# Interleaving the recurrent heads more densely with the input projection, with three rows of the working buffer laid out anew

## The reference, cut to what matters

```python
h = _rmsnorm(x, mix_norm_gain[l])
proj = h @ w_in[l]                                   # 1696 RWKV columns, 1536 attention columns
p_rwkv, p_attn = proj[..., :RWKV_COLS], proj[..., RWKV_COLS:]
y_rwkv = _rwkv7_mixer(p_rwkv, ...)                   # 8 heads of 64, a recurrence over the tokens
q, k, v = (t.reshape(B, S, ATTN_HEADS, HEAD_DIM) for t in jnp.split(p_attn, 3, axis=-1))
q = _partial_rotary(q, positions)
k = _partial_rotary(k, positions)
o = _dilated_attention(q, k, v)                      # 8 heads of 64, causal, three dilated patterns
o = _rmsnorm(o, ...)
x = x + jnp.concatenate([y_rwkv, y_attn], axis=-1) @ w_out[l]
```

## Time and profile before

| | us |
|---|---|
| median of three runs (3556.31 to 3567.62) | 3562.47 |
| the profiled execution, its own time | 3562.47 |
| its span, first to last instruction | 3560.6 |
| TensorE busy in it | 3266.1 (92%) |
| VectorE busy | 1754.1 (49%) |
| ScalarE busy | 1186.1 (33%) |
| mean granted clock of TensorE, as a share of 2.4 GHz | 0.958 |
| projection, second half, to the last tile's step | 1933.5 to 2222.3 |
| rest of the heads, to the first matmul of the output projection | 2222.3 to 2731.3 |

### The profile page before, as it was taken

How to read it: one execution, slowest core, us unless ns; L and a number is a source line. 1 busy time by engine, 2 the same in 40 slices (tenths; PEclk the granted TensorE clock), 3 DMA queues, 4 the chain that set the end, 5 groups by cost and what they waited for, 6 DMA issues and landing times.

```text
span 3560.6 us, 55136 instructions
## 1 busy us (share of the span) xinstructions
PE 3266.1 (92%) x23686; PEld 2719.5 (76%) x23686; DVE 1754.1 (49%) x2930; ACT 1186.1 (33%) x2048; POOL 262.9 (7%) x234
## 2 busy tenths in 40 slices
PE   5999888889989999999889999878888999999998
PEld 4887767778878888888677776767676878888887
DVE  6646443246565243435664545445555653434355
ACT  4232354452453221213443313343424431212133
POOL 1121010012130000000120000000001100000000
PEclk8999899999989999999999999989989999999999
DMA  2111112114423111113444212110002222111123
GB/s 100 66 64 52 63 70 77 66 54 137 137 89 117 55 44 52 41 60 113 136 160 131 72 57 79 37 37 20 19 20 72 89 95 66 48 48 51 50 90 112
DMA packets 85236, 262.29 MB, mean 74 GB/s; under 512 B 10209, under 2 KB 10337, under 8 KB 84865
## 3 DMA queue, kind: packets, MB, share of 16 engines
q1 hardware_dynamic: 73056, 217.78, 18.6%
q0 software_dynamic: 7040, 23.16, 1.9%
q10 hardware_dynamic: 4896, 17.84, 1.2%
HBM read 216.51 MB, written 42.21 MB: 73 GB/s over the span
## 4 chain that ended last, share of the span: by engine, by line
PE 75%; DVE 14%; ACT 6%; issue 3%; DMA 2%; POOL 1%; SPq 0%; ACTq 0%; DVEq 0%; POOLq 0%
PE ps L127 72%; PE ps L130 2%; DVE w_lo L161 1%; DVE m_S L171 1%; ACT w_hi L158 1%; ACT L140 1%; DVE HB L161 1%; DVE HB L171 1%; PE ps L126 1%; ACT m_D L140 1%; DVE r_t L161 1%; DVE r_in L161 0%; DVE extra L161 0%; DVE C L171 0%; DMA w_raw<-in_w_u 0%
## 5 line engine op out<-in xcount | busy, mean ns | idle before, releaser
L161 DVE TENSOR_TENSOR w_lo<-w_raw,w_hi 128x1024 fp32r<-128x1024 f32 (+3 forms) x353 | 398.4, 1129 | 386.0 <-ACT w_hi L158 382.4
L127 PE MATMUL ps<-XHA,w_hi 128*128 128x264 f32 (+3 forms) x1456 | 477.8, 328 | 32.6 <-ACT m_G L140 8.8
L127 PE MATMUL ps<-XLA,w_hi 128*128 128x264 f32 (+3 forms) x1456 | 465.8, 320 | 0.0
L127 PE MATMUL ps<-XHA,w_lo 128*128 128x264 f32 (+3 forms) x1456 | 463.9, 319 | 0.0
L158 ACT ACTIVATE w_hi<-w_raw 128x1024 fp32r<-128x1024 f32 (+3 forms) x353 | 339.9, 963 | 337.6 <-PE ps L127 281.3
L127 PE MATMUL ps<-XHB,w_hi 128*128 128x512 f32 x920 | 380.2, 413 | 8.5 <-POOL XLB L161 5.5
L127 PE MATMUL ps<-XLB,w_hi 128*128 128x512 f32 x920 | 363.2, 395 | 0.0
L127 PE MATMUL ps<-XHB,w_lo 128*128 128x512 f32 x920 | 363.0, 395 | 0.0
L127 PEld LDWEIGHTS ps<-XHA,w_hi 128*128 128x128 f32 x1456 | 284.3, 195 | 65.2 <-issue 26.3
L127 PEld LDWEIGHTS ps<-XLA,w_hi 128*128 128x128 f32 x1456 | 284.7, 196 | 21.8 <-issue 4.1
L127 PEld LDWEIGHTS ps<-XHA,w_lo 128*128 128x128 f32 x1456 | 284.7, 196 | 16.7
(11 more groups left out here) (452 smaller groups left out, 6219.6 us busy)
## 6 DMA issues: line engine op xcount, KB each, us to landing
w_raw<-in_f_gate SPq DMA_DIRECT2D x66, 512.0 KB, 3.3
w_raw<-in_f_up SPq DMA_DIRECT2D x66, 512.0 KB, 3.3
w_raw<-in_w_out SPq DMA_DIRECT2D x32, 512.0 KB, 3.3
w_raw<-in_f_down SPq DMA_DIRECT2D x48, 320.0 KB, 2.9
w_raw<-in_f_down SPq DMA_DIRECT2D x32, 384.0 KB, 3.1
w_raw<-in_w_rkv SPq DMA_DIRECT2D x24, 512.0 KB, 3.4
w_raw<-in_w_attn SPq DMA_DIRECT2D x24, 512.0 KB, 4.0
w_raw<-in_w_qkvo SPq DMA_DIRECT2D x16, 512.0 KB, 3.3
```

The lines of the kernel that those rows point to most:

```text
L127: return Issued(e.matmul(out, a, b, start=start, stop=stop))
L161: return Issued(self.eng and self.eng.tensor_tensor(out, a, b, op))
```

## The change

- `BESIDE` goes from 0.41 to 0.55. The same 208 slots of the second projection half then issue 114 steps of the braid and not 85 (208 x 0.55 = 114.4, 208 x 0.41 = 85.3).
- The output of `gd2` of the first half lies in row 5 of `HB` and not in row 7, the staging buffers `K.pS2` in rows 6 and 7 and not in rows 5 and 6.
- The waits go with the rows: in `in3_dve` for the stores of `h2` (rows 6 and 7 before the first staging, rows 0, 2, 4 and 5 before the lora outputs); in `attention_act` ACT waits for the lora products of both streams' second units ahead of pair 1, where it waited ahead of pair 3. The wait ahead of pair 0, for row 4, stays.
- `BLOCKS`, the order of the query blocks, was 0 to 7 and is written out as such; it issues the same instructions.

```diff
-BESIDE, BEG, ATT = 0.41, 6, 2
+BESIDE, BEG, ATT = 0.55, 6, 2
...
     if c:
         return K.HB[rows, 0 if rows.stop <= 64 else 2, 512:1024]
-    return K.HB[rows, 4 if rows.stop <= 64 else 7, 0:512]
+    return K.HB[rows, 4 if rows.stop <= 64 else 5, 0:512]
...
             n3_over(V, K)
-            for row in (5, 6):
+            for row in (6, 7):
                 V.wait_ge(K.hs[row], ("h2", 1))
...
-            for row in (0, 2, 4, 7):
+            for row in (0, 2, 4, 5):
                 V.wait_ge(K.hs[row], ("h2", c))
...
-BLOCKS = tuple(range(8))
-UNITS = [(i, h) for i in BLOCKS for h in range(2)]
+UNITS = [(i, h) for i in range(8) for h in range(2)]
...
-            i = BLOCKS[u // 2]
+            i = u // 2
...
     for j in range(4):
-        for g in range(2 if j in (0, 3) else 0):
+        for g in range(2 if j < 2 else 0):
             A.wait_ge(K.rws[g].pe, ("g", 1) if j else ("a", 1))
...
-        K.pS2 = [K.HB[:, 5 + n // 2, 512 * (n % 2):512 * (n % 2) + 512] for n in range(4)]
+        K.pS2 = [K.HB[:, 6 + n // 2, 512 * (n % 2):512 * (n % 2) + 512] for n in range(4)]
```

## The result

The changed kernel takes 3619.44 us (median of four runs, 3619.04 to 3627.52), the kernel before 3561.53 beside it: 57.9 us slower, a ratio of 1.0168 with a 95% interval of 1.0146 to 1.019. I had forecast slower, by 17.7 us, and a range up to 3604. The sign was right; the size was not, and neither was the range.

What follows compares the result with a forecast made beforehand. TensorE, busy for 92% of the span, was taken to bound the kernel. Projection +56.4, middle -19.2, attention alone -22.5 and clock +3 gave +17.7 us on 3562.5, so 3580, with a range of 3562 to 3604.

Steps and rivals of the forecast that it cites:

- The rows and the wait: New rows of `HB` and ACT's wait moved ahead of pair 1: claimed to cost nothing.
- Attention alone at full clock: Last stretch, attention's last 29 steps without RWKV: 61 us against 83.5, or -22.5 us, before any clock cost.
- I take +3: Last stretch: time at TensorE's lower clock would cost 6 us against 3 now, so +3 us.
- the tail at the lower clock: Rival: attention alone at 1.2 GHz, up to 25 us on top; 0.22 together with stalls beside the projection, about 3600 us.
- idle time that I leave unchanged because as many steps are issued: Middle, 133 steps of everything together: idle time stays 71.5 us, busy time falls 19.2, with 10 us either way.
- +56.4 for the projection: Second projection half with 29 more steps: 47.4 us of RWKV work plus 9 of idle time, 288.9 to 345.3 us.
- RWKV's moved work: Second stretch's TensorE busy time less attention's matmuls, 72.65 - 25.3 = 47.4 us, added to the projection half.
- I take 9: Idle time that 29 more steps bring beside the projection: 9 us, between bounds of 0 and 25.

Runs made afterwards that it cites:

- the density alone: The kernel before with only `BESIDE` raised to 0.55, rows of `HB` and waits as before: 3619.59 us, ratio 1.0167.
- the filling: The changed kernel with useless TensorE matmuls after scores of pair 3's blocks 2 to 7 and ahead of the closing transposes: 3599.45 us, ratio 1.0109.
- The pairs: The kernel before with steps beside the projection issued two at a time, 84 issued and not 85: 3609.41 us, ratio 1.0136.
- the thinner `w_lo`: Only 8 of 1024 columns of `w_lo` computed in the second projection half (wrong result): changed kernel 3621.27 us, kernel before 3548.47 us.

## Why the prediction missed

**Right.** The sign, and the balance behind it: TensorE's work is conserved, 29 steps move, attention's last 29 run alone. The rows and the wait (shown by the density alone). Attention alone at full clock: 61 us predicted, 58.4 measured with the filling.

**Wrong: "I take +3" for the clock.** It was the largest single miss of a term. Attention's matmuls there took 54.5 us for 36.4, and keeping TensorE busy gave 17.3 us back. I had put the granted clock at 0.85 from the stretches of before; it was 0.62. I had the right case among the rivals ("the tail at the lower clock") and gave it up to 25 us, but weighed the present 0.94 against it. That clock was the one of a stretch in which RWKV's matmuls filled the waits, and I was taking them out. The Trainium skill ("TensorE: Matmul & The Clock Gate", "HAM oscillation — how this bites in real kernels") puts the cost at half of the time at the lower clock. Here 2 x 0.38 x 75.7 = 57.5 us were at 1.2 GHz, so by it I estimate 28.8, and 17.3 were measured. The trace of the changed kernel shows most of the difference. The three pieces of this stretch at the lower clock, 57.1 us, hold 42.2 us in which TensorE was busy, and 14.9 in which it waited and so had nothing to lose:

```profile
2713.42:2737.31 23.89, 18.79 (x74) 0.50 0.00 1
2747.55:2757.79 10.24, 9.83 (x42) 0.50 0.00 0
2761.20:2784.16 22.96, 13.57 (x65) 0.50 0.02 4
```

Half of the busy part is 21.1 us. It does not hide behind DVE and ACT: the 17.1 us by which attention's matmuls grew, counted once, are nearly all of the 17.3. What makes 17 of the 21 was not looked into.

**Wrong: "idle time that I leave unchanged because as many steps are issued"**, with 10 us either way. Idle time in the middle rose from 71.5 to 83.1 us, and the busy time fell by 15.5 and not 19.2. That makes 15.3 us. The runs with 84, 86 and 88 steps and with other distances of the streams show that the premise was false: which steps meet moves the stretches after the projection by up to 39 us at the same number of steps, and the kernel before holds the best pairing of those run. That the changed kernel's 15.3 us are of this kind is likely, but not shown, and which operations collide in a bad pairing was not found.

**Too small: +56.4 for the projection.** It was 69.7, and the 13.3 us missing have two parts. The first is busy time: I put RWKV's moved work at 47.4 us, and busy time rose by 54.9. I had subtracted the sum of attention's three groups in the earlier trace rows, 25.3 us, but the groups overlap, and together they cover 22.6; that is 2.7 of the 7.5. The returns to the projection's matmuls, which no term of mine had, are 3.9. (The same slip in the last stretch, 36.4 for 33.9, is about the 2.6 us by which attention alone came out under my 61.) The second is the "I take 9" of idle time. It was 14.8, inside the bounds of 0 to 25. The pairs show that projection work between steps hides some of the waits; the thinner `w_lo` shows that 8.7 of the 31.1 us go when DVE has less of the projection's own work. The changed kernel's longest new wait, as a timeline of DVE, ends TensorE's idle time at 1948.81:

```profile
1941.30 0.43 DVE L167 TENSOR_SCALAR r_t<-r_t 128x512 f32<-128x512 f32 x1 [2.00 <-ACT r_t L140]
1943.20 0.69 DVE L161 TENSOR_TENSOR HB<-p_G 96x512 f32<-96x512 f32 x1 [1.48 <-ACT p_G L158]
1943.93 0.75 DVE L171 SCALAR_TENSOR_TENSOR HB<-HB,vecs,p_G 96x512 f32<-96x512 f32 x1
...
1946.32 1.23 DVE L161 TENSOR_TENSOR w_lo<-w_raw,w_hi 128x1024 fp32r<-128x1024 f32 x1 [1.64 <-ACT w_hi L158]
1947.46 0.48 DVE L167 TENSOR_SCALAR r_t<-r_in,vecs 128x512 f32<-128x512 f32 x1
1947.97 0.69 DVE L161 TENSOR_TENSOR r_t<-r_t 128x512 f32<-128x512 f32 x1
1948.81 1.19 PE L127 MATMUL ps<-r_t,cst 128*128 128x512 f32 x1 [6.00 <-DVE r_t L161]
```

No instruction in this trace writes `r_in` or `r_t` between 1941.73 and the first of RWKV's two operations at 1947.46, so both could have run over 4 us earlier. The token shift and `w_lo` were written ahead of them, and each first waited for ACT.

**The sum of the misses.** Projection 13.3, middle 15.3, last stretch 11.7 (17.3 - 3 for the clock, less 2.6 by which attention alone was shorter than 61), the profiles' 5.2 the other way: 35.1, from 17.7 to 52.8. **The range** was wrong for another reason: every unknown came out on its bad side (5.8 of 16 us for the idle time beside the projection, more than the 10 for the middle, 14.3 of 25 for the clock), and I had let only one of them do so at a time. They may have a cause in common, that less cover makes more waits; that waits lower the clock is shown for the last stretch alone. With their bad ends added, 17.7 + 16 + 10 + 25 would have reached 3631.

No version run here that does all of the work beats the kernel before. The best at 0.55 is the changed kernel with the last stretch filled, 3599.45 us.

## What to carry to other kernels

When work is moved away from beside a chain, size the chain's remainder at the lower clock first: the granted clock of a stretch belongs to the mixture that runs in it. Where two or more streams are interleaved by a fixed pattern, a change of one step can cost as much as the change under study, so time the neighbouring patterns before putting a difference down to amounts of work. And unknowns that may share a cause are to be added at their bad ends, not taken one by one. Where groups of a profile overlap, take what they cover together and not the sum of their times.

## What was not expected of the hardware

The lower clock came without a long wait. In the changed kernel it fell at 2713.42, after 13.7 us at the upper one in which no single wait of TensorE was over 1.5 us. Blocks 3 and 4 of the last pair then ran wholly at 1.2 GHz, while TensorE was busy for over three quarters of the time and no single wait was above 1.9 us:

```profile
2699.76:2713.42 13.66, 10.04 (x86) 1.00 0.00 1
2713.89:2722.90 9.01, 6.87 (x27) 0.50 0.00 0
2722.90:2733.70 10.80, 8.53 (x36) 0.50 0.01 2
```

And matmuls of no use made a kernel 20 us faster, which they did only where TensorE had nothing else to do. Ahead of the last transposes alone, in the kernel before, they changed nothing. Among other work the same means cost 6 and 10 us in two kernels, and in a third, the one with 84 steps, brought a gain too small to be told from none.
